# Second gate, layer-norm sums and first branch placed ahead of the 40 attention heads instead of between them

## What is computed

```python
a_in, q, k, v, qi, ki, wi, ga, gb = split_in(rms_norm(x, g_attn) @ w_in)
glu = a_in[..., :D_CONV] * jax.nn.sigmoid(a_in[..., D_CONV:])
h = layer_norm(causal_dwconv(concat(conv_past, glu), conv_w, conv_b), ln_g, ln_b)   # 31 taps
y_a = jax.nn.silu(h) @ w_a_out                      # first branch
o = attend(q, k, v, qi, ki, wi)                     # top-k attention, 8 heads
y_b = o.reshape(b, t, D_ATTN) @ w_b_out             # second branch
x = x + (jax.nn.sigmoid(ga) * y_a + jax.nn.sigmoid(gb) * y_b) @ w_o
...                                                 # then a gated ConvFFN
```

## Time and profile before

| | us |
|---|---|
| median of 3 runs | 1437.95 |
| lowest and highest | 1432.43, 1440.23 |
| the profiled execution | 1431.12 |
| its span in the trace | 1429.0 |
| PE busy in the span | 1266.1 (89%) |
| DVE busy | 752.9 (53%) |
| ACT busy | 286.2 (20%) |
| POOL busy | 204.6 (14%) |

### The profile page before, as it was taken

The page is one execution under the profiler, slowest core; times in us unless marked ns, Lnnn a source line. Parts: engine busy times, 40 slices in busy tenths (PEclk is TensorE's granted clock), DMA queues, the critical chain, the costliest instruction groups (busy, mean ns, idle before and its releaser), DMA issues. The chain is left out here.

```text
span 1429.0 us, 17511 instructions
## 1 busy us (share of the span) xinstructions
PE 1266.1 (89%) x7043; PEld 990.3 (69%) x7043; DVE 752.9 (53%) x1723; ACT 286.2 (20%) x526; POOL 204.6 (14%) x210
## 2 busy tenths in 40 slices
PE   6989999987886899879637989999999999999996
PEld 3556763335774677656314447788999999998996
DVE  5112134998889872976864231312766666661220
ACT  2122223110001001332202220022222222232111
POOL 0010000001001121363774410000000000000111
PEclk9989985999998899987667879999999999999998
DMA  5232320113030213453764610620233333222330
GB/s 170 89 122 67 140 73 1 41 43 102 1 118 1 104 49 98 132 172 119 211 203 124 236 30 32 181 62 0 60 89 89 89 89 89 80 61 76 103 108 27
DMA packets 107020, 131.54 MB, mean 92 GB/s; under 512 B 8095, under 2 KB 76087, under 8 KB 105894
## 3 DMA queue, kind: packets, MB, share of 16 engines
q1 hardware_dynamic: 91830, 80.21, 18.4%
q0 software_dynamic: 14384, 48.62, 11.0%
q10 hardware_dynamic: 725, 1.60, 0.4%
HBM read 124.86 MB, written 5.54 MB: 91 GB/s over the span
## 5 line engine op out<-in xcount | busy, mean ns | idle before, releaser
L707 PE MATMUL G<-xnT,wring 128*128 128x280 f32 x768 | 206.7, 429 | 11.0 <-DVE gluT L1387 11.0
L1173 PE MATMUL G<-xnH,whi 128*128 128x274 f32 x704 | 205.2, 291 | 0.7 <-DVE aext L1667 0.7
L1174 PE MATMUL G<-xnL,whi 128*128 128x274 f32 x704 | 203.5, 289 | 0.0
L1175 PE MATMUL G<-xnH,wlo 128*128 128x274 f32 x704 | 202.9, 288 | 0.0
L707 PEld LDWEIGHTS G<-xnT,wring 128*128 128x128 f32 x768 | 154.8, 205 | 49.9 <-DVE gluT L1387 11.4
L699 PE MATMUL G<-wring,xnT 128*128 128x512 f32 (+3 forms) x400 | 158.2, 552 | 0.7 <-ACT srel L1803 0.7
L1174 PEld LDWEIGHTS G<-xnL,whi 128*128 128x128 f32 x704 | 133.4, 189 | 0.1
L1173 PEld LDWEIGHTS G<-xnH,whi 128*128 128x128 f32 x704 | 132.4, 188 | 1.0 <-issue 0.9
L1175 PEld LDWEIGHTS G<-xnH,wlo 128*128 128x128 f32 x704 | 133.1, 189 | 0.0
L1628 DVE TENSOR_TENSOR wlo<-wraw,whi 128x2048 fp32r<-128x2048 f32 (+1 forms) x38 | 76.4, 2011 | 93.3 <-ACT whi L1936 92.6
L699 PEld LDWEIGHTS G<-wring,xnT 128*128 128x128 f32 (+1 forms) x400 | 66.6, 185 | 77.8 <-issue 76.8
(11 more groups left out here) (361 smaller groups left out, 1964.8 us busy)
## 6 DMA issues: line engine op xcount, KB each, us to landing
wraw<-in_w_up_dram SPq DMA_DIRECT2D x44, 512.0 KB, 5.2
wring<-in_w_in_dram SPq DMA_DIRECT2D x9, 2048.0 KB, 7.8
wraw<-in_w_down_dram SPq DMA_DIRECT2D x16, 704.0 KB, 4.6
qB<-scr_q SPq DMA_DIRECT2D x32, 256.0 KB
wring<-in_w_o_dram SPq DMA_DIRECT2D x2, 2048.0 KB, 8.7
toep<-scr_toep SPq DMA_DIRECT2D x1, 2432.0 KB, 9.2
wring<-in_w_in_dram SPq DMA_DIRECT2D x2, 1024.0 KB, 9.3
wring<-in_w_a_out_dram SPq DMA_DIRECT2D x1, 2048.0 KB, 8.0
```

Source lines behind the costliest of these rows:

```text
L707: last = pe.matmul(out[:, i, 0:b - a], w[:, j, c:c + P], x[:, j, a:b], start=(j == 0), stop=(j == k - 1))
L1173: pe.matmul(out, w_hi, x_hi, start=start, stop=False)
L1174: pe.matmul(out, w_hi, x_lo, start=False, stop=False)
L1175: return pe.matmul(out, w_lo, x_hi, start=False, stop=stop)
```

## The change

The eight `gb`, two `ln` and eight `ya` products stand in one block ahead of head 0, on PE, ACT and DVE alike. DVE makes all 62 taps in a row, then the norm steps with key products 0 to 2 between them, then each `ya` product's result followed by one key product (3 to 10). The heads come behind that with nothing between them but the decode tokens' work, whose steps stand at earlier heads; keys go at 3 for 2 heads. POOL waits for the last `ya` ahead of `hotk`, `tokB` and key 10. The key reduction is one instruction instead of two. On ACT the copy `pT` of head `a` stands ahead of the exponential of `a + 1` instead of behind it. SP's loads of query rows 3 to 31 stand behind the load of `ya`'s weights.

```diff
-    FILL = {2 * n: ("gb", n) for n in range(KM)}
-    FILL.update({30: ("ln", 0), 32: ("ln", 1)})
-    FILL.update({35 + n: ("ya", n) for n in range(5)})
...
+    products += [("gb", n) for n in range(KM)] + [("ln", 0), ("ln", 1)] + [("ya", n) for n in range(KM)]
+    products += [("at", a) for a in range(ATTEND)]
...
-    AT_QUADS = {18: 0, 20: 1, 22: 2, 24: 3, 29: 4, 31: 5, 33: 6, 35: 7}
+    AT_QUADS = {10: 0, 12: 1, 14: 2, 16: 3, 23: 4, 25: 5, 27: 6, 29: 7}
+    TAPS, KEYS_FIRST = (KC - PE_CONV) * CONV_W, 3 + KM
...
-        return min(NS, 4 * (a + 1) // 3)
+        return min(NS, KEYS_FIRST + 3 * (a + 1) // 2)
...
+            step(dve.tensor_reduce(lgat[:, g, :, col:col + 8], x[:, :, :].rearrange("p c (h d) -> p c h d", d=64), AX.X, ALU.add), S["qk_done"], free=True)
...
+        for i in range(TAPS):
+            conv_tap(i)
+        ready(dve, ("gb", KM - 1))
+        step(dve.memset(psT[:, :, :, :], 0.0), S["at_clear"])
+        norm_take(0)
+        for i in range(3):
+            key_product(i)
+        norm_take(1)
+        for n in range(KM):
+            branch_take(n)
+            key_product(3 + n)
...
+        for n in range(KM):
+            gate("gb", n)
+        norm_squares()
+        norm_silu()
...
-        ready(pool, ("gb", 3))
+        ready(pool, ("ya", KM - 1))
```

More of the change, by code:

```diff
@@ L635, in _ @@
                 ready(sp, ("cv", PE_CONV - 1))
-            if name == "ya":
+            if name == "yb":
                 for t in range(3, NS):
                     query_rows(t)
+                sp.wait_ge(S["pv_used"], 18)
+            if name == "wo0":
                 sp.wait_ge(S["hotk_used"], 2)
@@ L984, in norm_sums @@
             last.then_inc(g_ready, 1)
[L986 to L995, removed]
         def logits(a):
@@ L1110, in group_out @@
             last.then_inc(S["ov_ready"], 1)
+        for n in range(KM):
+            transposed(("gb", n), KM, 512, (n % 4) * P, xnT)
+        for stage in range(2):
+            norm_sums(stage)
+        pe.wait_ge(S["silu_done"], KC)
+        for n in range(KM):
+            transposed(("ya", n), KC, D_MODEL, n * P, hT)
         logits(0)
@@ L1130, in _ @@
                 group_out(AT_OUT[a])
-            if a in FILL:
-                fill(FILL[a])
         turn_out(NT - 1)
-        for n in range(5, KM):
-            fill(("ya", n))
         pe.wait_ge(S["ov_done"], 2)
@@ L1599, in _ @@
                 at_out(a // N_HEADS - 1)
[L1600 to L1609, removed]
             for i in range(keys_by(a - 1), keys_by(a)):
@@ L1613, in _ @@
                 hot_buckets(AT_HOT[a])
[L1614 to L1615 removed]
+            if a in AT_MAX:
+                group_max(AT_MAX[a])
             if a in AT_WEIGHTS:
@@ L1619, in _ @@
                 group_out(AT_OUT[a])
-        branch_take(4)
         at_out(NT - 1)
-        for n in range(5, KM):
-            branch_take(n)
         def low_weights(i):
@@ L1908, in _ @@
             _, rows, _, _ = att_tile(r)
[L1909 to L1913, removed]
             act.wait_ge(S["at_trans"], a + 1)
@@ L1921, in _ @@
             step(last, S["at_pT"], free=True)
+            if a + 1 < ATTEND:
+                at_exp(a + 1)
             if h == 0 and r:
@@ L1925, in _ @@
                 group_scale(AT_LOGITS[a])
+            if a in AT_MAX:
+                group_exp(AT_MAX[a])
             if a in AT_PROBS:
                 group_turn(AT_PROBS[a])
[L1928 to L1931, removed]
         take_out(NT - 1)
```

10 lines of the change are left out of this document (3 added, 7 removed).

## The result

| | before | after |
|---|---|---|
| median, us | 1435.19 (1431.47 to 1440.23, 4 runs) | 1460.05 (1457.33 to 1465.13, 4 runs) |
| span of the profiled execution, us | 1429.0 | 1455.4 |
| mean granted clock of TensorE | 0.913 | 0.893 |
| ratio to before | | 1.0175, 95% interval 1.0127 to 1.0223 |
| yb starts, us | 888.1 | 912.2 |

The kernel became slower by 25 us (forecast: 37 us slower, 1475, range 1450 to 1498).

A forecast was written before the change was run, and what follows sets the result against it. Decode tokens' gathers, started one at a time by GpSimd, bound the middle of the stretch. 557.9 + 134.6 + 99.2 + 133.4 = 925.1 against 888.1, 37.0 us longer, giving 1475 on the median; range 1450 to 1498.

The forecast's parts named there:

- Part A: From the first logits through the block of gate, norm and branch to a head's first maximum: 134.6 us.
- the estimate with ten slowed gathers: If only ten key products slowed gathers, 44 gathers take 63.6 instead of 65.5 us; 2 us left in the range.
- Part B: Heads 0 to 13 with 21 keys, first maximum to quad 2, set by GpSimd's gathers: 99.2 us.
- Part C: Heads 14 to 39, quad 2 to yb: 93.5 plus 37 for heads 14 to 21 plus 2.9 last output turn, 133.4 us.
- the 93.5: Rest of head 22 to head 39: 124.7 us in the kernel before, less 31.2 for norm sums, ya and norm wait.
- part C better: Heads 14 to 39 without fillers run at full clock: 10 to 20 us off, 1455 to 1465; within the forecast's 0.69.
- part C worse: Heads 14 to 39 stay at low clock and quads wait for values: 15 to 25 us more, 1490 to 1500; chance 0.15.

The follow-up runs named there:

- k1: The changed kernel with one gather per selected value instead of two (result differs, only time counts): ratio to before 1.0047.
- h1: The changed kernel with only gate and taps ahead; norm sums and branch back between heads 30 to 39, GpSimd waiting for the fourth gate product only: ratio to before 1.0082.
- e2: The changed kernel with keys 10 to 12 gathered ahead of the wait for the branch, and values 0 to 5 between keys 5 and 6: ratio to before 1.0130.
- e3: The changed kernel with ScalarE's old order, the exponential of head a+1 ahead of the copy pT of head a: ratio to before 1.0308.
- e4: The changed kernel with the sum of a key product in two instructions again: ratio to before 1.0325.
- e34: The changed kernel with both ScalarE's old order and two sums per key product: ratio to before 1.0324.
- b5: The kernel before with ScalarE's new order and one sum per key product, without the rearrangement: ratio to before 0.9887.
- h2: h1 with values 0 to 5 gathered early, behind key 15: ratio to before 1.0175.
- e1: The changed kernel with the gathers of keys 10 to 12 ahead of the wait for the eighth ya product: ratio to before 1.0179.
- b2: b5 with 24 of the 62 taps moved ahead of the first maximum, into VectorE's wait there: ratio to before 0.9900.

## Why the prediction was right, and where it was off

**The bound was read rightly.** "The decode tokens' gathers, which POOL starts one at a time, bound the middle of the stretch": k1 shows it (14.8 us for twelve gathers), and h1 shows that the stretch keeps its length wherever the block ends. What the prediction didn't see is how close the heads' own chain up to quad 0 lies behind that bound (e2, k1).

**Part A** was 134.6 us and measured 133.0 (556.56 to 689.55). Its running sum has a slip of 0.3 at the branch's end (647.7 + 30.9 + 1.7 is 680.3, not 680.6), and the estimate with ten slowed gathers has one of 0.1 (63.5, not 63.6); neither matters. Its terms held: the gate 62.0 forecast and 60.6 measured, the branch 30.9 and 33.3, POOL's release at 680.6 and 678.0, DVE's wait 8 to 9 and 8.7.

**Part B** was 99.2 and measured 101.8. Four gathers, as a pair of key and value needs, took 5.84 us in the stretch from 724.75 to 783.12, forty gathers, against the 5.96 forecast from the earlier trace rows. Of a pair's four gathers one usually took 1.6 to 1.95 and three 0.95:

```profile
748.33 1.68 POOL L2032 DMA_INDIRECT ksel<-in_cache_k_dram,gather_row  x1 [0.30 <-issue]
750.31 0.95 POOL L2032 DMA_INDIRECT ksel<-in_cache_k_dram,gather_row  x1 [0.30 <-issue]
751.57 0.95 POOL L2032 DMA_INDIRECT vsel<-in_cache_v_dram,gather_row  x1 [0.30 <-issue]
752.82 0.95 POOL L2032 DMA_INDIRECT vsel<-in_cache_v_dram,gather_row  x1 [0.30 <-issue]
```

The Trainium skill (GPSIMD Engine Reference, Specifications) says that GpSimd shares its SBUF interfaces with VectorE, with contention when a VectorE instruction has two SBUF inputs. This trace agrees so far as one long gather goes with each key product: the one of 1.68 above starts at 748.33, the product's two-input instruction at 747.96. The pace of 1.46 a gather is what the sum rests on either way.

But one sentence of part B was wrong, and the sum came right by luck: "Everything else of heads 0 to 13 hides under this: [...] the new order on ACT", and with it "the quads 0 and 1 at heads 10 and 12 run well ahead of values 6 and 10". Quad 0 was 2 us ahead of value 6, and only by both small edits; without either the stretch is 7 to 8 us longer, without both 10.5, and the total some 20 (e3, e4, e34). The merged sum I had valued at 0.1 us a key; it took 2.39 where the two took 2.71, 0.3 less, and a part of its effect lay in POOL's queue. The cover that I named was never priced: I didn't work out when quad 0 would come.

**Part C is the term that was mis-sized**: 133.4 forecast, 120.9 measured, and this 12.5 is the difference between +37 and +25. Of its three pieces the 93.5 for head 22's rest to head 39 held: head 22's weighted sum ends at 823.8, head 39's at 910.1, 86.3, and the two quads of 3.64 that the 93.5 had in it make 93.6, though not as forecast (see below). The wrong piece is "heads 14 to 21 [...] 37", priced at the low clock of the earlier trace rows. The timeline of PE, weighted sums of heads 15, 16 and 18 to 22:

```profile
797.25 0.95 PE L1011 MATMUL TB<-vnat,pT 128*128 128x64 f32 x4
...
800.51 1.38 PE L1011 MATMUL TB<-vnat,pT 128*128 128x64 f32 x6
...
811.16 0.78 PE L1011 MATMUL TB<-vnat,pT 128*128 128x64 f32 x6
...
816.13 0.78 PE L1011 MATMUL TB<-vnat,pT 128*128 128x64 f32 x6
818.34 0.88 PE L1011 MATMUL TB<-vnat,pT 128*128 128x64 f32 x6
820.44 0.78 PE L1011 MATMUL TB<-vnat,pT 128*128 128x64 f32 x6
823.02 0.78 PE L1011 MATMUL TB<-vnat,pT 128*128 128x64 f32 x6
```

From quad 2's start to head 22's weighted sum's end is 32.5, less two quads 25 us, not 37. Once the keys are in, nothing holds these heads. They follow one another at 2.1 to 2.6 us where I had 4.4, and from 808 on at the full 2.4 GHz. That is the rival "part C better", which I had named, and even priced (10 to 20 us), and put behind the low clock because the one head row that I had read of this tile was at the low clock.

**The rival "part C worse" came true too, in another place**, and is hidden in the 93.6. The heads of the last row tile, back to back:

```profile
884.21 1.44 PE L1011 MATMUL TB<-vnat,pT 128*48 128x64 f32 x10
885.59 0.74 PE L1000 MATMUL UB<-pack,pr 48*128 48x48 f32 x5
886.26 1.94 PE L984 MATMUL G<-kT,qT 64*48 64x512 f32 x2
888.13 0.62 PE L986 MATMUL G<-selb,identb 128*48 128x512 bf16 x1
888.68 0.34 PE L984 MATMUL G<-kT,qT 64*48 64x16 f32 x2
888.95 0.21 PE L986 MATMUL G<-selb,identb 128*48 128x16 bf16 x1
889.01 1.44 PE L1011 MATMUL TB<-vnat,pT 128*48 128x64 f32 x10
```

4.80 us a head at 1.2 GHz with no gap. The same weighted sum took 0.89 in the last head before, at 2.4 GHz with a product of the branch beside each head. What paid for it was not worked out term by term. The 93.5 also let the last value gathers "hold nothing back", and PE waited for them three times, 4.3, 2.0 and 2.6 us at quads 5, 6 and 7, the first of them here:

```profile
839.94 1.03 PE L1079 MATMUL UB<-vsel,psT 128*32 128x512 f32 x1 [4.25 <-DMA ksel<-in_cache_v_dram,gather_row]
```

So the 93.6 is right in size by luck.

**Of the marks that I set**: hotk near 681 (678.0), first maximum at 690 to 695 (689.6, 0.4 early), clock under 0.8 from 690 to 790 (0.50 and 0.53), gathers not under 1.3 (1.46), PE busy under half there (48.3 of 100 us), key product 31 near 790 (788.7), heads 14 to 39 not under 110 (120.9) held; yb at 915 to 945 missed by 3 us, and POOL's wait ahead of hotk was 8.8 us and not tens, since POOL was held up at keys 3 to 9 first (19.8 us at one of them).

**The change as a whole**, by the runs: the rearrangement alone costs 3.2% (e34), about 46 us, and the two small edits that came with it bring 1.5% back. In the kernel before, without the rearrangement, they bring 1.1% (b5). Against b5, which has the same small edits, the gate ahead costs 2.0% (h1, some 28 us) and norm sums and branch ahead another 0.9% (some 13 us).

## What to carry to other kernels

Work out not only when the engine that starts the gathers is released, but when each buffer it will ask for comes free, in the order of its queue: here one string of gathers had 2 us to spare at a single wait, and undoing either of two edits costed at nothing broke it and cost some 20 us, of which the profiles show 11 to 13 and that wait itself 8.6 and 9.8. When gathers are taken out of a string that bounds a stretch, ask what the next bound is: here it was the heads ahead of quad 0, for which POOL stood 5 and 8 us when twelve gathers were gone. Work that stands between small steps of another chain isn't overhead if a third engine needs that time anyway; moved into a block ahead, it stays as long and the third engine's time is added behind it. When a change bundles a large move with small edits, try the small ones by themselves on the kernel before.

## What I had not expected of the hardware

- A granted clock of 0.50 (1.2 GHz) for an engine that never stops: between 880.8 and 904.7 PE shows no idle time in the change, with the small matmuls of heads of 48 rows, and the clock stayed low until yb. Before, with a product of 16 matmuls of 280 columns beside each of the last five heads, it was 1.00.
- The clock isn't fixed by the program alone. The first 200 us, where all these kernels run the same program, were granted 0.96 in the profiles of before, the change, e2 and h2 and 0.91 or 0.92 in those of e1, h1, k1, e4 and b2. In e1, h1, k1 and e4 PE began the block 4.6 to 7.5 us later than in the change. Differences of that size need medians.
- One sum over 128x1024 in place of two over 128x512 saves 0.3 us of 2.7 from a key product's start to the next instruction.
